# Softmax maxima and biases of two maps or heads taken together in a hybrid diffusion trunk

## What is computed

```python
def diff_attention(q, k, v, lam):          # 4 heads, two maps each, width 32
    s = jnp.einsum('bqhcd,bkhcd->bhcqk', qb, k).astype(jnp.float32) * scale
    p = jax.nn.softmax(s, axis=-1)
    a = p[:, :, 0] - lam * p[:, :, 1]
    return jnp.einsum('bhqk,bkhe->bqhe', a.astype(v.dtype), v)

def mla_attention(q, k_nope, k_rope, v):   # 4 heads, one map each
    s = jnp.einsum(... q[..., :64], k_nope) + jnp.einsum(... q[..., 64:], k_rope)
    p = jax.nn.softmax(s.astype(jnp.float32) * scale, axis=-1)
    return jnp.einsum('bhqk,bkhe->bqhe', p.astype(v.dtype), v)
```

## Time and profile before

| | us |
|---|---|
| median of 3 runs | 2319.76 |
| the profiled execution | 2319.28 |
| its span, first to last instruction | 2317.5 |
| TensorE busy (matmuls) | 2285.5 (99%) |
| VectorE busy | 1261.0 (54%), 2128 instructions |
| ScalarE busy | 925.5 (40%) |
| GpSimd busy | 746.7 (32%) |

### The profile page before, as it was taken

One profiled execution on the slowest core, in us unless ns is written; L12 is line 12 of the kernel. 1 busy time (PEld: TensorE's weight loads), 2 busy tenths in 40 slices (PEclk: granted clock), 3 DMA queues, 4 the chain that ended last, 5 costly groups with the idle time before them and its releaser, 6 DMA issues.

```text
span 2317.5 us, 40511 instructions
## 1 busy us (share of the span) xinstructions
PE 2285.5 (99%) x17116; PEld 2060.3 (89%) x17116; DVE 1261.0 (54%) x2128; ACT 925.5 (40%) x1767; POOL 746.7 (32%) x498
## 2 busy tenths in 40 slices
PE   7999999999999999999999999999999999999998
PEld 5888898888989998998988879888889899899897
DVE  4436458644336763763763463685444467547456
ACT  3435346634335331331363352555442443223223
POOL 0331321111333544544422303120123435444442
PEclk9999999999999999999999999999999999999999
DMA  9313222223232324223242142222232332222211
GB/s 323 133 58 122 75 96 81 78 75 120 97 116 73 91 91 128 74 91 123 78 138 74 39 134 87 90 67 92 74 111 86 106 91 73 77 69 79 86 60 69
DMA packets 221907, 221.62 MB, mean 96 GB/s; under 512 B 10583, under 2 KB 191391, under 8 KB 221471
## 3 DMA queue, kind: packets, MB, share of 16 engines
q1 hardware_dynamic: 212999, 193.77, 26.2%
q10 hardware_dynamic: 8727, 25.27, 3.2%
HBM read 209.90 MB, written 9.11 MB: 95 GB/s over the span
## 4 chain that ended last, share of the span: by engine, by line
PE 92%; ACT 3%; DVE 3%; issue 1%; POOL 1%; DMA 0%; SPq 0%; POOLq 0%; DVEq 0%; ACTq 0%
PE ps L897 50%; PE ps L1028 12%; PE ps L1563 11%; PE ps L1485 4%; PE ps L1169 3%; PE ps L1186 2%; PE ps L917 1%; PE ps L1130 1%; PE ps L1145 1%; PE ps L993 1%; PE ps L1115 1%; PE ps L1151 1%; PE ps L1387 1%; PE ps L908 1%; POOL w_lo L856 1%
## 5 line engine op out<-in xcount | busy, mean ns | idle before, releaser
L856 POOL TENSOR_TENSOR w_lo<-raw,w_hi 128x512 fp32r<-128x512 f32 (+1 forms) x486 | 736.5, 1546 | 1548.8 <-ACT w_hi L1635 997.3
L897 PE MATMUL ps<-h_hi,w_hi 128*128 128x320 f32 (+2 forms) x2368 | 615.3, 312 | 0.0
L897 PE MATMUL ps<-h_lo,w_hi 128*128 128x320 f32 (+2 forms) x2368 | 607.0, 309 | 0.0
L897 PE MATMUL ps<-h_hi,w_lo 128*128 128x320 f32 (+2 forms) x2368 | 606.5, 309 | 0.0
L897 PEld LDWEIGHTS ps<-h_hi,w_hi 128*128 128x128 f32 x2368 | 412.7, 188 | 7.1 <-issue 4.6
L897 PEld LDWEIGHTS ps<-h_lo,w_hi 128*128 128x128 f32 x2368 | 413.4, 188 | 0.2
L897 PEld LDWEIGHTS ps<-h_hi,w_lo 128*128 128x128 f32 x2368 | 413.3, 188 | 0.0
L1635 ACT ACTIVATE w_hi<-raw 128x2048 fp32r<-128x2048 f32 (+2 forms) x110 | 203.8, 1852 | 268.5 <-PE ps L1563 94.7
L1563 PE MATMUL ps<-w_hi,a_hi 128*128 128x512 f32 x440 | 172.4, 392 | 0.6 <-POOL w_lo L856 0.6
L2659 DVE TENSOR_SCALAR conv<-u_pad,vcol 128x642 f32<-128x642 f32 x88 | 90.1, 1024 | 151.2 <-ACT u_pad L2072 149.6
L1563 PE MATMUL ps<-w_lo,a_hi 128*128 128x512 f32 x440 | 171.3, 389 | 0.0
(11 more groups left out here) (348 smaller groups left out, 3479.7 us busy)
## 6 DMA issues: line engine op xcount, KB each, us to landing
raw<-in_w_mod SPq DMA_DIRECT2D x44, 1024.0 KB, 5.2
raw<-in_w_up SPq DMA_DIRECT2D x88, 512.0 KB, 4.8
raw<-in_w_gate SPq DMA_DIRECT2D x32, 1024.0 KB, 5.3
raw<-in_w_in SPq DMA_DIRECT2D x16, 1024.0 KB, 5.2
raw<-in_w_down SPq DMA_DIRECT2D x16, 1024.0 KB, 5.0
w_br<-in_w_branch ACTq DMA_DIRECT2D x8, 1024.0 KB, 5.0
raw<-in_w_out SPq DMA_DIRECT2D x8, 1024.0 KB, 5.1
raw<-in_w_down SPq DMA_DIRECT2D x8, 768.0 KB, 4.4
```

Source lines behind the costliest of these rows:

```text
L856: ins = nc.gpsimd.tensor_tensor(w_lo[part_slot(li, s)][:, c0:c1], raw[HOME[u]][:, c0:c1], w_hi[part_slot(li, s)][:, c0:c1].bitcast(F32), A ...
L897: ins = mm(out, w_at(w_hl[wi]), at_(x_hl[xi]), start=first and q == 0, stop=final and q == 2)
```

## The change

`softmax_bias`, called once per map, is replaced by `both_bias`, called once per head in the differential stretch (for its two maps) and once per pair of heads, on the even step, in the latent stretch. It waits for the scores of both, takes both maxima and then both biases. With 640 keys the maxima are one reduction over a view of two rows of 640 columns (columns 128 to 767 of each half of four banks); with 128 keys they stay two reductions, without a wait between. The biases are always one operation on two columns, and its semaphore rises by two at once.

```diff
-                    def softmax_bias(a_, m2):
-
-                        _, t, h = HEADS[a_]
-                        nk = P * len(key_blocks(br, t))
-                        m = FIRST_MAP[a_] + m2
-                        ve.wait_ge(s_mm.sem, now(s_mm, m + 1))
-                        b = score_bank(m)
-                        col = slice(m % 8, m % 8 + 1)
-                        V.tensor_reduce(stat[:, 0, col], bank(b, P, P + nk), AX.X, ALU.max).then_inc(vstep.sem, 1)
+                    def both_bias(m, nk):
+
+                        ve.wait_ge(s_mm.sem, now(s_mm, m + 2))
+                        both = ps[:, 0:4 * BANK].rearrange("p (a n) -> p a n", a=2)[:, :, P:P + nk]
+                        cols = slice(m % 8, m % 8 + 2)
+                        if nk > BANK:
+                            ins = V.tensor_reduce(stat[:, 0, cols], both, AX.X, ALU.max)
+                        else:
+                            for a in range(2):
+                                ins = V.tensor_reduce(stat[:, 0, m % 8 + a:m % 8 + a + 1], both[:, a], AX.X, ALU.max)
+                        ins.then_inc(vstep.sem, 1)
                         ve.wait_ge(vstep.sem, step())
-                        ts(stat[:, 1, col], stat[:, 0, col], -SCALES[br], None, ALU.mult).then_inc(bias_done.sem, 1)
+                        ts(stat[:, 1, cols], stat[:, 0, cols], -SCALES[br], None, ALU.mult).then_inc(bias_done.sem, 2)
...
-                        if i < 4 * T and br == 1:
-                            if i % 2 == 0:
-                                pair_bias(i)
-                        elif i < 4 * T:
-                            for m2 in range(2 if br == 2 else 1):
-                                softmax_bias(head0 + i, m2)
+                        if i < 4 * T and br == 1 and i % 2 == 0:
+                            pair_bias(i)
+                        if i < 4 * T and (br == 2 or br == 3 and i % 2 == 0):
+                            both_bias(FIRST_MAP[head0 + i], P * len(key_blocks(br, HEADS[head0 + i][1])))
```

## The result

| | runs | median us | lowest to highest |
|---|---|---|---|
| before | 20 | 2319.74 | 2318.88 to 2321.68 |
| after | 20 | 2324.78 | 2321.94 to 2327.96 |

The account below looks back on a forecast made before the run. TensorE, busy 99%, was taken as the bound. Later second exponentials in the differential stretch would cost 3.1 us over two layers, the latent stretch give back 0.3: 2.7 us slower than 2319.76, so 2322.5 us, range 2319.3 to 2325.0.

Follow-up runs that it names:

- experiment 3: The changed kernel with the two biases written by two one-column operations in place of one two-column operation: 2324.67 us, ratio 1.0019 to the kernel before.

## What to carry to other kernels

Taking two small reductions in one operation saved VectorE 8 us here and cost latency to whoever waits for the first result; where TensorE is busy 99% and waits only for the last link of a chain, ask how far each consumer moves, not how much the engine saves. When operations are merged, look for each new shape under what else runs at that time: here the merged one was held where the single one wasn't, and its price was the rest of another engine's instruction. And before two profiles are subtracted, compare their granted clocks.

## What the runs showed of the hardware

- A VectorE tensor_scalar of two float32 columns per partition, SBUF to SBUF, that starts under a GpSimd tensor_tensor (about 1.3 us each) ended 0.02 to 0.03 us behind that instruction, and took from 0.22 to 1.03 us (12 of 12 in the changed kernel). The same operation on one column took at most 0.16 us under the same work (26 in the kernel before, 28 in experiment 3), and the reciprocal of two columns was not held either (8 under GpSimd's work in the changed kernel, 0.17 us, as elsewhere).
- Twenty matmuls of two columns in a row, 2.3 us, were followed in some executions by 3.4 us of granted clock 0.50, up to 1.7 us lost each time. With 128 columns for 0.1 us more the profiles of the five kernels that have them show none there, where seven of the eight others have one to three, and the kernel before is 1.7 us faster in its median.
